# Expert choice in a two-block fp32 model: gathered rows, slot tokens, and a ring of four weight pieces

## The reference

```python
def expert_choice_ffn(n, w_router, w_gate, w_up, w_down):
    cap = EC_FACTOR * L // N_EXPERTS                       # 64
    logits = jnp.einsum('bld,de->ble', n, w_router).astype(F32)
    aff = jax.nn.softmax(logits, axis=-1)
    vals, idx = lax.top_k(jnp.swapaxes(aff, 1, 2), cap)
    xs = jax.vmap(lambda hb, ib: hb[ib])(n, idx)
    a = jnp.einsum('becd,edf->becf', xs, w_gate)           # 1024 -> 512
    u = jnp.einsum('becd,edf->becf', xs, w_up)
    y = jnp.einsum('becf,efd->becd', jax.nn.silu(a) * u, w_down) * vals[..., None].astype(n.dtype)
    return jax.vmap(lambda yb, ib: jnp.zeros((L, D), yb.dtype).at[ib.reshape(-1)].add(yb.reshape(-1, D)))(y, idx)
```

## Time and profile before

| | us |
|---|---|
| median of 3 runs | 3813.19 (3798.38 to 3815.2) |
| the profiled execution's own time | 3801.55 |
| its span | 3799.5 |
| TensorE busy | 3334.2 (88%) |
| VectorE busy | 1218.9 (32%) |
| ScalarE busy | 564.0 (15%) |
| mean granted TensorE clock | 0.924 |

### The profile page before, as it was taken

One profiled execution on the slowest core, in us unless ns is written; L12 is line 12 of the kernel. 1 busy time (PEld: TensorE's weight loads), 2 busy tenths in 40 slices (PEclk: granted clock), 3 DMA queues, 4 the chain that ended last, 5 costly groups with the idle time before them and its releaser, 6 DMA issues. The chain is left out here.

```text
span 3799.5 us, 39217 instructions
## 1 busy us (share of the span) xinstructions
PE 3334.2 (88%) x15257; PEld 2049.7 (54%) x15257; DVE 1218.9 (32%) x2141; ACT 564.0 (15%) x1062; POOL 198.4 (5%) x170
## 2 busy tenths in 40 slices
PE   7997888989897999699888999998997949999895
PEld 3334688864444332288664788546874624444342
DVE  4663566674413011337223000002732131111013
ACT  2113233322200111110220000001013010000000
POOL 0000111023200000000010000000001000000000
PEclk9997799999997899899898999998997969999997
DMA  5110000001052199512020222302202062357926
GB/s 140 70 44 0 10 1 0 0 34 45 12 229 89 68 379 375 211 59 89 0 89 11 77 77 74 136 0 78 84 22 89 0 247 73 142 199 285 418 102 241
DMA packets 111898, 408.49 MB, mean 108 GB/s; under 512 B 10627, under 2 KB 13059, under 8 KB 102212
## 3 DMA queue, kind: packets, MB, share of 16 engines
q1 hardware_dynamic: 101756, 385.62, 26.5%
q10 hardware_dynamic: 7752, 13.30, 1.6%
q0 software_dynamic: 2304, 8.39, 0.6%
HBM read 380.36 MB, written 26.93 MB: 107 GB/s over the span
## 5 line engine op out<-in xcount | busy, mean ns | idle before, releaser
L1918 PE MATMUL proj<-feat,w 128*128 128x264 f32 x1920 | 435.7, 390 | 7.6 <-PE proj L1918 3.2
L1918 PEld LDWEIGHTS proj<-feat,w 128*128 128x128 f32 x1920 | 366.6, 192 | 75.8 <-issue 10.6
L2629 PE MATMUL pgu<-gu,xg 128*64 128x320 f32 (+1 forms) x2560 | 394.0, 463 | 7.3 <-POOLq L2572 6.4
L2310 PE MATMUL pp<-feat,w 128*128 128x264 f32 x1408 | 316.6, 389 | 6.0 <-DMA w<-in_ffn_up 6.0
L2310 PEld LDWEIGHTS pp<-feat,w 128*128 128x128 f32 x1408 | 269.6, 192 | 52.7 <-issue 6.1
L2629 PEld LDWEIGHTS pgu<-gu,xg 128*64 128x64 f32 x2560 | 181.1, 138 | 205.5 <-issue 129.2
L296 PE MATMUL proj<-feat,w 128*128 128x512 f32 x576 | 255.6, 600 | 14.1 <-ACT padded L317 13.0
L2636 PE MATMUL py<-down,hm_t 128*64 128x512 f32 x880 | 200.1, 603 | 8.3 <-POOLq L2572 8.3
L1987 DVE SCALAR_TENSOR_TENSOR conv<-glu,cols,conv x240 | 184.4, 768 | 44.7 <-DVE conv L1987 43.2
L296 PEld LDWEIGHTS proj<-feat,w 128*128 128x128 f32 x576 | 107.8, 191 | 161.6 <-issue 130.1
L344 DVE SCALAR_TENSOR_TENSOR mixed<-padded,taps,mixed 128x512 f32<-128x512 f32 x216 | 162.3, 751 | 28.7 <-DVE mixed L341 0.9
(11 more groups left out here) (378 smaller groups left out, 3872.3 us busy)
## 6 DMA issues: line engine op xcount, KB each, us to landing
gu<-in_moe_gu SPq DMA_DIRECT2D x16, 3072.0 KB, 13.6
w<-in_w_in SPq DMA_DIRECT2D x23, 2048.0 KB, 7.9
gu<-in_moe_gu SPq DMA_DIRECT2D x16, 2560.0 KB, 16.0
wg<-in_w_gate SPq DMA_DIRECT2D x16, 2048.0 KB, 12.3
wu<-in_w_up SPq DMA_DIRECT2D x16, 2048.0 KB, 17.5
wd<-in_w_down SPq DMA_DIRECT2D x16, 2048.0 KB, 14.9
down<-in_moe_down SPq DMA_DIRECT2D x8, 3072.0 KB, 18.1
w<-in_ffn_up SPq DMA_DIRECT2D x22, 1024.0 KB, 4.7
```

The lines of the kernel that those rows point to most:

```text
L1918: last = pe.matmul(proj[:, slot, half, 0:HALF], w[:, b, c, k * P:(k + 1) * P], core.feat[:, k, half * HALF:(half + 1) * HALF], start=k == ...
L2310: last = pe.matmul(pp[:, b, a, half, 0:HALF], w[:, b, a, k * P:(k + 1) * P], core.feat[:, k, half * HALF:(half + 1) * HALF], start=k == 0, ...
L2629: last = pe.matmul(pgu[half(h), part, 0:n], xg[:, k, :], w[:, k, h, :], start=k == 0, stop=k == DK - 1)
```

## The change

Five things change together.

1. The normalised rows are stored to HBM (`choice_rows`, four DMAs issued by ACT in `rms_to_features`), and each pair's 128 rows are fetched by one indirect DMA of POOL, two pairs ahead, into `slot_rows` (two buffers). PE transposes them in two halves (`turn_rows`), one beside gate and one beside up of the pair before, and ACT copies them scaled to `xe` (two buffers). The 64 matmuls with `hot`, and `picked_t`, are gone.
2. `hot` is now the stationary operand of small matmuls with the token numbers and affinities (`mark`, 17 columns) as the moving one: `found` has the token and the affinities of each slot (L1485). A pair's scatter matrix is one comparison of that token with 0 to 511 (`pick`), made in the loop; the affinity is applied as a scale per partition where ACT copies `ye`. The matmuls into `pb` and the `scatter` matrices are gone.
3. The logits have the 16 router columns as the stationary operand, and the four token tiles go to four groups of 32 partitions of `pr`; one transposition turns them back.
4. The weights are laid out on the host so that a partition's part of a matrix is 16 KB in one piece, and go through a ring of four buffers of 4 MB; a piece is the gate, up or down matrices of one pair. The first four are asked for at the start of `rms_to_features`.
5. The pairs are written out in place of the loop. Pair j-1 is spread in two halves, one between up of pair j and the transposition of its product, one between this transposition and down. PE itself waits for the end of each gate, up and down before it counts the piece as used.

The diff, cut to what the sentences above and the steps of the prediction speak of:

```diff
                 act.wait_ge(stats, 1)
                 act.activation(stat[:, 2, :], stat[:, 1, :], ACT.Sqrt).then_inc(root, 1)
+                if store is not None:
+                    for t in range(TILES):
+                        act.wait_ge(scaled, t + 1)
+                        act.dma_start(store[t * P:(t + 1) * P, :], scaled_rows[:, t, :]).then_inc(stored, 16)
...
+        self.src = [A[name] for name in ("w_gate", "w_up", "w_down")]
+        self.ring = core.sb(ctx, "ring", [P, self.RING, 2, DK * FF])
...
+    def load(self, sp, n):
+        j, kind = divmod(n, 3)
         for e in range(2):
...
+            sp.dma_start(self.ring[:, n % self.RING, e, :], self.src[kind][2 * j + e]).then_inc(self.landed[n % self.RING], 16)
...
+    def first_loads(self, sp):
+        for n in range(self.RING):
+            self.load(sp, n)
+
+    def wait(self, pe, n):
+        pe.wait_ge(self.landed[n % self.RING], 32 * (n // self.RING + 1))
...
+    def gather(self, pool, j):
+        pool.indirect_dma_start(out=self.rows[:, j % 2, :], out_offset=None, in_=self.src,
+                                in_offset=bass.IndirectOffsetOnAxis(ap=self.index[:, j:j + 1], axis=0)
+                                ).then_inc(self.gathered[j % 2], 16)
...
+            @block.gpsimd
+            def _(pool):
+                pool.wait_ge(choice.stored, 16 * TILES)
+                pool.wait_ge(choice.found, 1)
+                for j in range(2):
+                    choice.gather(pool, j)
...
-                pe.wait_ge(landed, 48)
-                for t in range(TILES):
-                    for k in range(DK):
-                        last = pe.matmul(logits[:, t, :], core.feat[:, k, t * P:(t + 1) * P], wr[:, k, :],
+                pe.wait_ge(landed, 32)
+                for k in range(DK):
+                    for t in range(TILES):
+                        last = pe.matmul(pr[Q * t:Q * t + NE, 0:P], wr[:, k, :], core.feat[:, k, t * P:(t + 1) * P],
                                          start=k == 0, stop=k == DK - 1)
                 last.then_inc(p_sem, 1)
-                pe.wait_ge(v_sem, 5)
+                pe.wait_ge(lt_out, TILES)
+                pe.transpose(pl[:, 0:P], lt[:, :], ident).then_inc(p_sem, 1)
+                pe.wait_ge(v_sem, AFF)
                 for t in range(TILES):
                     last = pe.transpose(pt[0:NE, t * P:(t + 1) * P], aff[:, t, :], ident)
...
-                for j in range(PAIRS):
-                    if j >= 2:
-                        pe.wait_ge(b_out, j - 1)
-                    pe.matmul(pb[:, j % 2, 0, :], spread[:, j, :], slot[:, :], start=True, stop=True)
-                    pe.matmul(pb[:, j % 2, 1, :], spread[:, j, :], aff_e[:, :], start=True, stop=True).then_inc(b_made, 1)
...
-                    for half in range(2):
-                        if k:
-                            pe.wait_ge(x_out, (k - 1) * 2 + half + 1)
-                        for t in range(TILES):
-                            last = pe.matmul(px[:, half, :], core.tok[:, t, k * P:(k + 1) * P],
-                                             hot[:, t, half * BANK:(half + 1) * BANK], start=t == 0, stop=t == TILES - 1)
-                        last.then_inc(x_made, 1)
+                for t in range(TILES):
+                    pe.wait_ge(hot_made, t + 1)
+                    for j in range(PAIRS):
+                        last = pe.matmul(found[:, j, :], hot[:, t, j * P:(j + 1) * P], mark[:, t, :],
+                                         start=t == 0 and j == 0,
+                                         stop=t == TILES - 1 and j == PAIRS - 1)
+                last.then_inc(p_sem, 1)
...
+                for t in range(TILES):
+                    dve.tensor_copy(lt[Q * t:Q * t + NE, :], pr[Q * t:Q * t + NE, 0:P]).then_inc(lt_out, 1)
+                dve.wait_ge(p_sem, 2)
...
-                dve.tensor_copy(aff_e[:, :], pt[0:NE, :])
...
-                for j in range(PAIRS):
-                    dve.wait_ge(b_made, j + 1)
-                    do(dve.tensor_scalar(scatter[:, j, :], pb[:, j % 2, 0, :], place, None, ALU.is_equal))
-                    dve.tensor_tensor(scatter[:, j, :], scatter[:, j, :], pb[:, j % 2, 1, :], ALU.mult).then_inc(b_out, 1)
...
+                dve.wait_ge(p_sem, 5)
+                dve.tensor_copy(choice.index[:, :], found[:, :, 0]).then_inc(choice.found, 1)
+                do(dve.tensor_copy(choice.token[:, :], found[:, :, 0]))
+                do(dve.tensor_tensor(owned[:, :, :], found[:, :, 1:], route.own, ALU.mult))
+                do(dve.tensor_reduce(choice.value[:, :], owned[:, :, :], AX.X, ALU.add))
...
+                for n in range(weights.RING, weights.PIECES):
+                    sp.wait_ge(used, n - weights.RING + 1)
+                    weights.load(sp, n)
...
+                for j in range(2, PAIRS):
+                    pool.wait_ge(turned, 2 * (j - 2) + 2)
+                    choice.gather(pool, j)
...
+                def turn_rows(j, half):
+                    pe.wait_ge(choice.gathered[j % 2], 16 * (j // 2 + 1))
+                    if j or half:
+                        pe.wait_ge(x_out, 2 * j + half)
+                    for k in range(HK):
+                        c = (half * HK + k) * P
+                        last = pe.transpose(px[:, k * P:(k + 1) * P], choice.rows[:, j % 2, c:c + P], ident)
+                    last.then_inc(turned, 1)
+
+                def expand(j, kind, out, made):
+                    weights.wait(pe, 3 * j + kind)
+                    w = weights.piece(3 * j + kind)
+                    for k in range(DK):
                         for e in range(2):
...
+                            rows = slice(e * CAP, (e + 1) * CAP)
+                            last = pe.matmul(out[rows, :], xe[:, j % 2, k, rows], w[:, e, k, :], start=k == 0, stop=k == DK - 1)
+                    last.then_inc(made, 1)
+                    pe.wait_ge(made, j + 1)
+                    pe.sem_inc(used, 1)
+
+                def spread(j, half):
+                    pe.wait_ge(sc_made, j + 1)
+                    pe.wait_ge(y_out, 2 * j + half + 1)
+                    for t in range(TILES):
+                        n = (2 * j + half) * TILES + t
+                        if n >= 2:
+                            pe.wait_ge(o_read, n - 1)
+                        pe.matmul(po[:, n % 2, :], sc[:, j % 2, t * P:(t + 1) * P], ye[:, half * BANK:(half + 1) * BANK],
+                                  start=True, stop=True).then_inc(o_made, 1)
+
...
                     pe.wait_ge(t_out, j + 1)
...
+                    if j:
+                        pe.wait_ge(y_out, 2 * j)
...
+                    pe.wait_ge(y_made, 2 * j + 2)
+                    pe.sem_inc(used, 1)
...
+                for half in range(2):
+                    turn_rows(0, half)
+                for j in range(PAIRS):
+                    pe.wait_ge(x_out, 2 * j + 2)
+                    if j:
+                        pe.wait_ge(silu, j)
+                    expand(j, 0, pg, gate_made)
+                    if j + 1 < PAIRS:
+                        turn_rows(j + 1, 0)
+                    if j:
+                        pe.wait_ge(h_made, j)
+                    expand(j, 1, pu, up_made)
+                    if j + 1 < PAIRS:
+                        turn_rows(j + 1, 1)
+                    if j:
+                        spread(j - 1, 0)
+                    pe.wait_ge(h_made, j + 1)
+                    for f in range(FB):
+                        last = pe.transpose(pt[:, f * P:(f + 1) * P], hid_e[:, f * P:(f + 1) * P], ident)
+                    last.then_inc(t_made, 1)
+                    if j:
+                        spread(j - 1, 1)
+                    contract(j)
+                for half in range(2):
+                    spread(PAIRS - 1, half)
 
...
+                def rows_out(j, half):
+                    act.wait_ge(turned, 2 * j + half + 1)
+                    for k in range(HK):
+                        f = half * HK + k
+                        last = act.activation(xe[:, j % 2, f, :], px[:, k * P:(k + 1) * P], ACT.Copy,
+                                              scale=core.cols[:, COL_NORM2 + f:COL_NORM2 + f + 1])
+                    last.then_inc(x_out, 1)
...
+                        act.wait_ge(y_made, 2 * j + half + 1)
+                        if j:
+                            act.wait_ge(o_made, (2 * j - 1 + half) * TILES)
+                        act.activation(ye[:, half * BANK:(half + 1) * BANK], py[:, half, :], ACT.Copy,
+                                       scale=choice.value[:, j:j + 1]).then_inc(y_out, 1)
...
+                def pick(j):
+                    if j >= 2:
+                        dve.wait_ge(o_made, (j - 1) * 2 * TILES)
+                    dve.tensor_scalar(sc[:, j % 2, :], route.tokens, choice.token[:, j:j + 1], None, ALU.is_equal).then_inc(sc_made, 1)
```

(32 more changed lines are left out.)

205 lines of the change are left out of this document (90 added, 115 removed).

## The result

The changed kernel took 3701.8 us (median of 4 runs, 3694.83 to 3718.29) beside 3810.47 for the kernel before on the same chip: ratio 0.9726, 95% interval 0.9684 to 0.9767. Measured again, in five runs, it took 3705.82 (ratio 0.975, 0.9727 to 0.9773).

A forecast was written before the change was run, and what follows sets the result against it. It took PE's chain with idle time, the transfers close behind, and 58 us of PE-only matmuls as bounds. From 3801.55 us, -66.0 to the first gate and -18.0 in the block gave 3717.5, plus 11.6 3729; range 3708 to 3756.

The forecast's parts named there:

- logits: Routing: 64 records in four 16-column groups, with copies and a transposition, take 8.6 us for 12.9; -4.3 us.
- slots' transposition to first gate: Routing: `found`, a gather and transpositions replace the matmuls with `hot`; 27.1 us in place of 88.7, -61.6 us.
- block: First gate to final norm: eight pairs of 31.6 us plus 3.3 once, 256.1 us for 274.1; -18.0 us.
- spreading stays paced by DVE: Expert pair: DVE's additions at 0.69 us each set the spreading's pace, 7.6 us per pair.
- DMA share below 1 in the later pairs: Expected profile sign in the expert block, together with no wait of PE for a piece.
- With the 11.6 of the median: Whole kernel: the median of the old runs lies 11.6 us above the profiled execution, so 3717.5 becomes 3729 us.
- (a): Expert block: the weight stream bounds the loop, the last piece 3 to 12 us late; 3732 to 3741 us, chance 0.15.
- (b): Before the first gate: gather (+12 us) or ACT's issues (+5) cost their upper bounds; 3741 to 3746 us, chance 0.13.
- (c): Expert pair: PE gains nothing, through waits or a falling clock; 34.1 us per pair, +20, 3749 us, chance 0.12.
- (d): Expert pair: PE gains more, its own waits hidden and banks free; 30.3 us per pair, -10, 3719 us, chance 0.12.
- (e): Expert block: slower than before because the stream falls below 260 GB/s; 3832 us, chance 0.01.
- (f): Weight ring: no prefetch since its first use comes late; only shifts a part of (a), no chance of its own.

The follow-up runs named there:

- run 3: The changed kernel with the logits' 64 records issued group by group instead of interleaved across the four groups; 3715.12 us in one execution.
- run 4: The changed kernel with the weights in the old order of HBM (runs of 2 KB), ring and all else kept; median 3735.9 us, ratio 0.9824.
- run 2: The changed kernel with the logits in their old form (16 moving columns, no groups, no second transposition); median 3715.99 us.
- run 9: The changed kernel with two pairs' spreading summed in PSUM before DVE adds it, so half the additions; median 3712.41 us.
- run 1: The changed kernel profiled once more without an edit; the final norm began at 1488.5 us and what followed took 2225.7 us.
- run 6: The changed kernel with each pair's spreading put behind its own down again, as in the kernel before; median 3723.4 us, ratio 0.9768.
- run 5: The changed kernel with weights in the old order of HBM and the first four pieces issued in the routing block; median 3698.38 us, ratio 0.9728.

## Why the prediction missed

**The mechanism was right, several terms were mis-sized.** From the features' start to the final norm, forecast and measured by the first profile:

| step | forecast | measured |
|---|---|---|
| ACT's stores, ahead of `feat` | +0.5 | -0.5 |
| logits | -4.3 | -9.1 |
| `aff_e` | -0.6 | -0.6 |
| slots' transposition to first gate | -61.6 | -62.5 |
| block | -18.0 | -22.5 |
| sum | -84.0 | -95.2 |

*Logits.* The step "with 128 columns at the lower clock I take 0.10, so 6.4 us; bounds 0.06 and 0.199" failed, in the rate and in the clock, and its lower bound with it: 0.030 us per record at a clock of 1.00 (run 3's and the changed kernel's alike), 0.056 at 0.50 (run 4, 3.61 us). Of the 4.5 us between 6.4 and 1.94, 2.8 are the rate and 1.7 the clock. The row that the step started from, 0.141 at 512 moving columns, gives 0.035 at 128 when it is scaled by its columns alone, and 0.07 at half the clock, which the prediction didn't work out. Run 3 shows that the groups' lying beside each other is a factor of 3.0 in it; run 2 that the old form in its place would have cost 6.7 us more at the first gate.

*Slots to first gate.* Right within 0.9 us, in part by luck, since its parts cancel: `found` 13.84 us for 12.7, the gather 4.3 for 6.0 (1226.63 to 1230.94).

*Block.* The pair's sum of 31.6 was too large: it took 31.0, eight times 0.6 less. Gate, up, down and their waits took 22.2 (forecast 21.6), the transpositions 1.5 (2.0), the spreading 7.3 (7.6), and the 0.4 for ends was nothing. Nor does a change between tiles of 64 and 128 columns show a cost where PE doesn't wait: up begins at 1394.36, and the transpositions before it have their modelled end at 1394.43. The first gate took 8.62 as forecast. That "spreading stays paced by DVE" was wrong as a cause; run 9 shows PE. The stream gave 430 GB/s for the 418 taken, and PE waited for no piece, not even with three. It has little to spare, though: a pair's 13.1 MB take 30.5 us at that rate, beside a period of 31.0, and the sign "DMA share below 1 in the later pairs" did not come (1.01 up to 1400 us). The figure of about 358 GB/s (the Trainium skill, DMA: Bandwidth & Descriptors, Bandwidth) is, by the same section, what a core gets when both cores of its HBM domain stream; here one core runs, and 430 is above it. The Trainium skill (Perfetto Trace Analysis, Roofline) has some 435 for a single active core, and with that the trace agrees.

**From the sum to the time.** "With the 11.6 of the median" was the other step that failed. It took three runs of before for its median. Over the 40 runs of before in this study the median is 3805.9 (3786.6 to 3816.4), 4.4 above the profiled execution. Of the 27.2 us between 3729 and 3701.8, 11.2 are the terms above, 7.3 this median, and 4.0 the first four runs of the changed kernel against all nine (3705.8). 4.7 are left, and their cause stays open; in the two profiles of the changed kernel the features begin 3.6 and 2.2 us earlier than in that of before, but over all fourteen profiles this start scatters from 1172.4 to 1178.5 us. The medians of 40 and 9 runs differ by 100.1 us, the two profiles of the changed kernel by 98.8 and 97.6 from that of before at the final norm. The first two profiled executions as wholes differ by 83.3 us (3801.55 and 3718.29). That this is near the forecast 84.0 is luck: behind the final norm the changed one took 15.3 us longer, at the lower clocks shown in run 1.

**Slips in the working.** The recorded bounds don't follow from the terms: with those given for ACT's issues, the logits and the gather the sum runs from 3724 to 3752, where the text has 3713 to 3755 and 3708 to 3756 without a working. The logits' terms add up to 8.4, not 8.6. And of the four changes of tile width in an old pair three, not two, fell in idle time.

**The rivals.** (a) fell: no wait for a piece in any run at this pace, at 412 GB/s neither. (b) fell: 4.3 us, and 6.9 beside a stream. (c) fell; run 6 shows that undoing the order alone gives back 1.8 of 3.1 us. (d) is the side to which the case went, half of the way from 31.6 to its 30.3, but not for the first reason that it gave: PE's own waits did not hide, and taking them away gave 1.24 more. (e) and (f) had nothing for them. The dearest thing that the runs found was in none of them: SP's issuing of the first pieces ahead of a barrier, which the turned weights keep at 4.6 us and the old layout made 37.0 (runs 4 and 5).

## What to carry to other kernels

A transfer that is hidden can still cost on the engine that issues it: look at the issuing queue's own durations, and at the next barrier that waits for that engine. Before you name the engine that paces a pair of engines, compare the length of each one's records with that of like records elsewhere in the trace, where nothing holds them up. And measure a change by the stretch that it touches: here that repeats within 0.5 us, while the whole time scatters by 30 us with the clock of stages that the change doesn't touch.

## What the runs showed of the hardware

- Two attention stages of the same records took 145.1 to 174.9 us together, at granted clocks from 0.86 and 0.81 down to 0.64 and 0.64. What decides it between executions stays open.
- 16-column stationary tiles in four groups, 128 moving columns: 0.030 us per record interleaved and 0.092 group by group at clock 1.00, 0.056 interleaved at 0.50. The same product with 128 stationary and 16 moving columns: 0.11 at 1.00, 0.20 at 0.50.
- Two transfers of 2 MB each took SP 0.8 to 1.7 us to issue with runs of 16 KB, and 7.4 to 15.4 us with runs of 2 KB when others were under way (1.0 for the first two).
- A gather of 128 rows of 4 KB was there, and PE at work on it, 4.3 us after its issue began with quiet queues and 6.9 beside the last of the first pieces; over all eight gathers, most of them within the stream, the median to landing was 10.6.
- PE without its own waits ran 120 us at 100% busy, with the stream at 430 GB/s beside it.
